# An attention stage on one Trainium2 core: turning the summed values with two stacked identities instead of one identity

## What is computed

```python
    p = jnp.exp(s - m[..., None])
    den = jnp.sum(p, axis=-1)
    if sinks is not None:
        den = den + jnp.exp(sk - m)
    o = jnp.einsum('ngrbqk,nbkgd->nbqgrd', p, vb.astype(jnp.float32))
    o = (o / den.transpose(0, 3, 4, 1, 2)[..., None]).reshape(n, L, G, R, hd)
```

## Time and profile before

| | |
|---|---|
| median of three runs | 3151.39 us (3147.83 to 3151.80) |
| the profiled execution | 3153.93 us, span 3152.2 us |
| granted TensorE clock, mean | 0.993 |
| TensorE busy | 3048.0 us, 97% |
| VectorE busy | 2063.1 us, 65% |
| ScalarE busy | 1468.7 us, 47% |
| GpSimd busy | 1202.5 us, 38% |
| the attention stage | from about 724 us to about 1595 us of the span |

### The profile page before, as it was taken

How to read it: one execution, slowest core, us unless ns; L and a number is a source line. 1 busy time by engine, 2 the same in 40 slices (tenths; PEclk the granted TensorE clock), 3 DMA queues, 4 the chain that set the end, 5 groups by cost and what they waited for, 6 DMA issues and landing times. The chain is left out here.

```text
span 3152.2 us, 44863 instructions
## 1 busy us (share of the span) xinstructions
PE 3048.0 (97%) x16138; PEld 2482.5 (79%) x16138; DVE 2063.1 (65%) x3931; ACT 1468.7 (47%) x2657; POOL 1202.5 (38%) x840
## 2 busy tenths in 40 slices
PE   8999999999888999999999999999999999999998
PEld 8888888887767766766678778888888788888887
DVE  5565565556768977877744687777555477777343
ACT  5332443236767866666633444444434344444332
POOL 2444244310000024442110198888110688885010
PEclk9999999999999999999999999999999999999999
DMA  4464545376666623431144522221565222223553
GB/s 142 163 187 144 176 156 172 124 209 224 240 222 240 184 69 83 134 89 43 61 114 126 170 87 81 90 84 67 187 218 186 97 83 92 81 80 113 185 196 107
DMA packets 274811, 433.90 MB, mean 138 GB/s; under 512 B 125760, under 2 KB 178240, under 8 KB 261568
## 3 DMA queue, kind: packets, MB, share of 16 engines
q1 hardware_dynamic: 265600, 395.70, 38.1%
q0 software_dynamic: 8992, 35.33, 3.4%
HBM read 312.51 MB, written 126.84 MB: 139 GB/s over the span
## 5 line engine op out<-in xcount | busy, mean ns | idle before, releaser
L1111 PE MATMUL z_banks<-ops,z_area 128*128 128x512 f32 x1720 | 434.1, 391 | 3.2 <-DVE z_area L858 3.2
L3194 PE MATMUL f_banks<-f_wt 128*128 128x512 f32 x1776 | 406.1, 389 | 0.0
L3194 PEld LDWEIGHTS f_banks<-f_wt 128*128 128x128 f32 x1776 | 333.3, 188 | 69.2
L1111 PEld LDWEIGHTS z_banks<-ops,z_area 128*128 128x128 f32 x1720 | 322.9, 188 | 70.3 <-DVE z_area L858 3.6
L2564 POOL TENSOR_TENSOR f_wt<-f_wt_f,f_wt 128x1024 fp32r<-128x1024 f32 x132 | 316.1, 2418 | 64.6 <-ACT f_wt L2695 59.1
L2043 ACT ACTIVATE w_small<-w_small,a_stats 128x128 f32<-128x128 f32 (+3 forms) x510 | 256.2, 516 | 90.5 <-DVE a_stats L2128 63.2
L3165 PE MATMUL f_banks<-low,f_wt 128*128 128x512 f32 x704 | 274.0, 389 | 0.0
L2986 DVE SCALAR_TENSOR_TENSOR near<-w_small,vk,near 128x1024 f32<-128x1024 f32 x88 | 231.2, 2628 | 1.7
L2128 DVE CUSTOM_DVE_ANT_0 w_small<-a_s_ps,near 128x128 f32<-128x128 f32 (+2 forms) x456 | 164.5, 392 | 89.2 <-PE a_s_ps L1929 79.1
L1973 PE MATMUL a_ot_ps<-a_turned_w,vs 128*64 128x256 f32 (+3 forms) x1452 | 221.3, 428 | 0.0
L3165 PE MATMUL f_banks<-f_oo,f_wt 128*128 128x512 f32 x704 | 217.0, 390 | 2.5 <-ACT kc_f L2729 1.2
(11 more groups left out here) (306 smaller groups left out, 7079.4 us busy)
## 6 DMA issues: line engine op xcount, KB each, us to landing
low<-z_parts SPq DMA_DIRECT2D x46, 1024.0 KB, 6.2
f_wt_f<-in_w_ffn SPq DMA_DIRECT2D x74, 512.0 KB, 4.1
z_area_f<-in_w_z SPq DMA_DIRECT2D x54, 512.0 KB, 5.1
f_raw_f<-in_w_ffn SPq DMA_DIRECT2D x22, 1024.0 KB, 4.8
f_wt_f<-in_w_ffn SPq DMA_DIRECT2D x22, 1024.0 KB, 5.3
g_up<-near SPq DMA_DIRECT2D x44, 512.0 KB, 2.6
f_wt_f<-g_up SPq DMA_DIRECT2D x88, 256.0 KB, 4.3
z_parts<-z_st_hi SPq DMA_DIRECT2D x68, 256.0 KB, 2.3
```

What stands on the lines that cost most here:

```text
L1111: last = pe.matmul(banks[:, bank, :], w[:, c * P:(c + 1) * P], rows[:, c * 512:(c + 1) * 512], start=(first and c == 0 and q == 0), stop=( ...
L3194: last = pe.matmul(banks[:, 2 * t + n, :], g[:, tok], w[:, n, :], start=(d == 0 and x == 0), stop=(d == NF - 1 and x == 2))
```

## The change

The even and odd partial sums are no longer turned as they are and added on VectorE or GpSimd. A constant `both` of 128 by 64 holds two identities of 64 by 64, one under the other. `turn_out` multiplies each 128 queries of `ot` with it, which gives in one product the sum of both halves with queries as lines: 64 columns for each tile, 256 for a group, the first half of the bank `on_ps` (`on_sum`). Kind k keeps its transposition. `finish` reads `on_sum`: kind b copies it, kind c multiplies it once, kinds w and s scale 256 columns into an `add` of half the width, and GpSimd adds one time.

```diff
-    steps = {"b": 1, "c": 3, "w": 2, "s": 2, "k": 5}
+    steps = {"b": 1, "c": 2, "w": 2, "s": 2, "k": 5}
...
-        add = sb("add", [P, 4, 2 * HD])
+        add = sb("add", [P, 4, HD])
+        both = sb("both", [P, HD])
...
+        on_sum = on_ps[:].rearrange("p i q -> p (i q)")[:, 0:4 * HD].rearrange("p (i d) -> p i d", d=HD)
...
-                pool.tensor_tensor(rows, rows, add[:, :, 0:HD], ALU.add).then_inc(upper_added, 1)
-                pool.wait_ge(upper_added, g - late + 1)
-                pool.tensor_tensor(rows, rows, add[:, :, HD:2 * HD], ALU.add).then_inc(out_done, 1)
+                pool.tensor_tensor(rows, rows, add[:], ALU.add).then_inc(out_done, 1)
...
                 w = out_width(g)
-                for i in range(4):
-                    last = pe.transpose(on_ps[:, i, 0:w], ot[0:w, i * P:(i + 1) * P], idt[0:w, 0:w])
+                if kind[g // 4] == "k":
+                    for i in range(4):
+                        last = pe.transpose(on_ps[:, i, 0:w], ot[0:w, i * P:(i + 1) * P], idt[0:w, 0:w])
+                else:
+                    pe.wait_ge(both_set, 2)
+                    for i in range(4):
+                        last = pe.matmul(on_sum[:, i, :], ot[:, i * P:(i + 1) * P], both[:], start=True, stop=True)
                 last.then_inc(out_turned, 1)
...
             dve.memset(blank[:], 0.0).then_inc(blank_set, 1)
+            for half in (slice(0, HD), slice(HD, P)):
+                dve.tensor_copy(both[half, :], idt[half, half]).then_inc(both_set, 1)
...
-                    dve.tensor_reduce(rows[:, :, 0:HD], halves, AX.X, ALU.add).then_inc(out_done, 1)
+                    dve.tensor_copy(rows[:, :, 0:HD], on_sum).then_inc(out_done, 1)
...
-                    dve.tensor_reduce(rows[:, :, 0:HD], halves, AX.X, ALU.add).then_inc(chain, 1)
+                    dve.wait_ge(chain, at + 1)
+                    dve.reciprocal(coef[:], coef[:]).then_inc(chain, 1)
                     dve.wait_ge(chain, at + 2)
-                    dve.reciprocal(coef[:], coef[:]).then_inc(chain, 1)
-                    dve.wait_ge(chain, at + 3)
-                    dve.tensor_tensor(rows[:, :, 0:HD], rows[:, :, 0:HD], coef[:].unsqueeze(2).to_broadcast([P, 4, HD]),
+                    dve.tensor_tensor(rows[:, :, 0:HD], on_sum, coef[:].unsqueeze(2).to_broadcast([P, 4, HD]),
                                       ALU.mult).then_inc(out_done, 1)
...
-                    dve.tensor_tensor(add[:], on_ps[:], coef[:].unsqueeze(2).to_broadcast([P, 4, 2 * HD]),
+                    dve.tensor_tensor(add[:], on_sum, coef[:].unsqueeze(2).to_broadcast([P, 4, HD]),
                                       ALU.mult).then_inc(added, 1)
```

More of the change, by code:

```diff
@@ L1654, in attend @@
         blank_set = sem("blank_set")
-        upper_added = sem("upper_added")
+        both_set = sem("both_set")
         scored = sem("scored")
@@ L2136, in finish @@
                 u, on, at32 = g // 4, on_ps[:, :, 0:HD + 1], (4 * g) % 32
-                halves = on_ps[:].rearrange("p i (h d) -> p i d h", h=2)
                 den = stats[:, at32:at32 + 4, 0:1]
```

## The result

| | before | changed |
|---|---|---|
| median of four runs | 3150.65 us | 3199.78 us (3196.4 to 3201.01) |
| ratio to before | 1 | 1.0156 (95%: 1.0144 to 1.0168) |
| span of the profiled execution | 3152.2 us | 3199.0 us |
| granted TensorE clock, mean | 0.993 | 0.993 |

The changed kernel is 49 us or 1.6% slower; the prediction was 3202 us with 3172 to 3220 as its range.

A forecast was written before the change was run, and what follows sets the result against it. TensorE, busy 97% of the span, was taken as the bound, with VectorE close to full only in kind c. 22 (b) + 8 (c) + 21 (w and s) = 51 us more gave 3202 us, range 3172 to 3220.

The forecast's parts named there:

- The price of a turning: TensorE, each group: eight records 0.113 us apart, 0.90 us, replace four transpositions of 0.44 us; 0.46 us more.
- The count of records: TensorE: each full float32 product is two weight loads and two passes, eight records a group, 960 in the profile after.
- Kind b: Attention, 48 groups: the whole 0.46 us adds in the closed loop, VectorE's 0.27 saving falls into idle time; 22 us more.
- The loop of the earlier trace: One kind b group, turning to turning: 4.81 us instead of 4.35, with VectorE idle about 0.9 us before its first bias.
- Kind c: Attention, 24 groups, both engines even: 0.46 us less VectorE's lateness of 0.15, taken as 0.33 each; 8 us more.
- Kinds w and s: Attention, 48 groups with TensorE the bound: nearly all of the added turning time shows; 21 us more.
- The sum: Whole kernel: 22 + 8 + 21 = 51 us more, median 3202 us, 1.6% slower.
- The clock: TensorE clock at its high level all along, 0.99 to 1.00 of 2.4 GHz; nothing of the price hangs on it.
- Pauses that swallow a part: Rival: TensorE's pauses and shorter VectorE work hide much of the price; only 23 us more, 3174 us; chance 0.22.
- A dearer product: Rival: 0.14 us a record, 0.68 us more a group, 82 us in all, 3233 us; chance 0.08.
- Four loads for each product: Rival: 16 records a group, 1.32 us more each, 158 us in all, 3310 us; chance 0.02.
- A gain from 64 columns: Rival: records paced by 64 columns, 0.055 us or less, so VectorE's kind c saving counts; about 3142 us; chance 0.05.

The follow-up runs named there:

- double: Kernel before the change, but each group of kinds b, c, w and s is turned twice into the same bank, eight transpositions instead of four; 3198.14 us.
- reduced: Changed kernel with the product in float32r, one weight load and one pass each, the sums losing their low bits; 3143.42 us.
- padded: Changed kernel with VectorE's saved time given back by copies of the bank to a spare tile ahead of each group's output; 3200.71 us.
- only_c: Kernel before the change, with the new product made only in the 24 groups of kind c; 3156.84 us.
- wide: Changed kernel with the constant 128 columns wide, so each product streams 128 moving columns instead of 64; 3200.92 us.

## Why the prediction was right

The forecast of 3202 us has 3199.78 beside it, and its steps can be held one by one against the runs.

- **The price of a turning**, 0.46 us from eight records 0.113 apart: measured 0.40 as a burst and 0.44 behind a wait, records 0.111 apart, and 0.34 to 0.43 in the mean from turning to turning. The count of records, which carried the sum, was exact (960), and `double` and `reduced` show that it is the count that costs: eight transpositions cost 3198.14, four float32r products of the same shape 3143.42.
- **Kind b**, 22 us: 48 x 0.42 = 20 us at full clock. The column says 20.7 for 45 turnings, which is nearer to 22 by luck: 10 us of half clock lie in it, against 3 to 4 in before. The loop of the earlier trace rows was foretold at 4.81 us and is 4.81; VectorE's idle time at about 0.9 and is 0.93. That the saving of VectorE falls into it is shown by `padded`.
- **Kind c**, 8 us: 8.2 from turning to turning, in the changed kernel and in `only_c` (the 9.1 of the column hold three turnings of kind b). Here the size was near and the reason was partly wrong. I credited VectorE's 0.68 us with 0.13 for each group, since VectorE had been late by 0.15 in the earlier trace rows. `double`, in which VectorE does all of its old work, pays 0.35 for a turning of kind c where the changed kernel pays 0.34, and `padded` 0.36. At most 0.02 of the credit was there. What made the sum come out is that the eight records cost less in this stream than reckoned: in the kernel before the next load follows the first of the turning's after 0.56 us (1021.12 to 1021.68), not after 0.44, and at the same place in the changed one after 0.89 (1042.90 to 1043.79), which is 0.33 more. A price put too high and a credit that was not there met, and that is luck. The group of the earlier trace rows grew from 4.41 to 4.76 us in the changed kernel.
- **Kinds w and s**, 21 us: 48 x 0.43 = 21 us (21.9 in the column, with a stretch of half clock). TensorE is the bound, and nearly all of it shows. ScalarE's wait for turned weights, 128.6 us before, is 146.0 after, in the waits from 1130 to 1645 us, where the same stretch lies:

```profile
ACT a_turned_w L2037 <- PE a_t_ps L1940: 146.0, 77, 7.8
```

- **The sum**, 51 us: 49 by the medians and by the turnings at full clock, 52.5 within the stage of the profiled execution. The range held.
- **The clock.** I read 0.99 to 1.00 in the earlier trace rows as the high level all along, with nothing of the price hanging on it. The medians' 49 us is what the turnings at full clock give, so the sum took no harm. But the mean of a long window hid two stretches of 3 to 4 us at 1.2 GHz, at the start of the stage and around 976 us, and in single traces such stretches differ by as much as the smaller effects of this study.
- **The rivals.** Pauses that swallow a part: no stretch shows more than 0.1 us of a turning. A dearer product (0.14 a record): 0.111. Four loads for each product: two. A gain from 64 columns: `wide` has 128 and costs 0.03 us more for a turning at most. In `reduced`, with half the records, a gain of 7 us does appear, but about 1 us of it is VectorE's. The table of the Trainium skill ("TensorE: Matmul & The Clock Gate", section "Back-to-back issue gap") gives about 60 cycles up to 64 columns and 134 for 128, but for an isolated product; the same section says that in a stream of loads and products both set the spacing. By the table alone `wide` would have been clearly dearer than the changed kernel. It is not: this case's records, each with new weights of 128 columns, agree with the second statement.

What stays open: why the load behind four float32r products comes 0.12 us sooner than behind four transpositions, and why TensorE's clock falls to half for 10 us in one trace and not at all in another. The prediction had no term for either; together they are a few us.

## What to carry to other kernels

Before work is moved to TensorE, count its records in a row of the same type and shape: a product in full float32 is two loads and two passes, and with new weights of 128 columns for each product the loads set the pace, with 64 columns streamed as with 128. A step that shortens an engine that waits earns next to nothing (1 us for 42 us of VectorE here), and a step that lengthens an engine in the closed loop costs nearly its whole length, also where that engine shows pauses: look whether the pause lies inside the same loop. Before two stretches of single traces are compared to the us, look at the granted clock in windows of a few us. Where the low bits can be spared, float32r turned the same change from 49 us of loss to 7 us of gain.

## What the runs showed of the hardware

- With new weights of 128 by 128 each time, loads start 0.11 us apart in all three forms: full float32 products ((0.97 - 0.19)/7), transpositions ((0.90 - 0.14)/7 in `double`) and float32r products ((0.53 - 0.19)/3). 64 or 128 moving columns differ by 0.03 us at most for the eight records of a turning in full float32.
- Loads of 64 columns that alternate between the two column halves start 0.027 us apart in the mean, in pairs, a quarter of a load of 128 columns. I had expected half.
- Going over from products on all columns to products on half the columns, the loads stand idle for 0.17 us for which the profile names no wait, and 16 half products take 0.61 us from first load to the next whole load although their own loads are through in 0.55. So half products pay where many stand together, not as an inlay.
- The granted clock falls to 1.2 GHz behind a wait of TensorE of 2.3 us in most traces, for 3 to 10 us, while TensorE is busy; in two of the traces it stays at 2.4 GHz behind the same wait.
